# A delta-rule stage with copies, updates and weight pieces in another order on ScalarE and VectorE

## What is computed

```python
def even_mixer(h, w_in, conv_a_w, dn_conv_w, a_log, dt_bias, dn_norm_w, w_out):
    p = h @ w_in
    a_gate_in, a_gate_out, a_h, qkv, z, beta_raw, alpha_raw = jnp.split(p, splits, -1)
    y_a = a_gate_out * causal_dwconv(a_gate_in * a_h, conv_a_w)
    qkv = jax.nn.silu(causal_dwconv(qkv, dn_conv_w))
    ...
    beta = jax.nn.sigmoid(beta_raw.astype(jnp.float32))
    g = -jnp.exp(a_log) * jax.nn.softplus(alpha_raw + dt_bias)
    o = gated_delta_rule(padw(q), padw(k), padw(v), padw(beta), padw(g))[:, pad:]
    ...
def gated_delta_rule(q, k, v, beta, g):
    ...
    t_mat = a_strict + jnp.eye(c, dtype=jnp.float32)
    sol = lax.linalg.triangular_solve(t_mat, rhs, left_side=True, lower=True, unit_diagonal=True)
    def step(s, inp):
        v_new = u_n - jnp.einsum('bhcd,bhde->bhce', w_n, s)
        o = jnp.einsum('bhcd,bhde->bhce', qd_n, s) + jnp.einsum('bhij,bhje->bhie', qk_n, v_new)
        s = s * gl_n[..., None, None] + jnp.einsum('bhcd,bhce->bhde', kd_n, v_new)
```

## Time and profile before

| | us |
|---|---|
| median of 3 runs | 1295.26 |
| lowest and highest | 1292.99, 1295.29 |
| the profiled execution | 1298.23 |
| its span, first to last instruction | 1296.4 |
| busy: PE, DVE, ACT, POOL | 1257.5, 883.4, 666.7, 183.6 |
| mean granted clock of PE | 0.981 |

### The profile page before, as it was taken

How to read it: one execution, slowest core, us unless ns; L and a number is a source line. 1 busy time by engine, 2 the same in 40 slices (tenths; PEclk the granted TensorE clock), 3 DMA queues, 4 the chain that set the end, 5 groups by cost and what they waited for, 6 DMA issues and landing times.

```text
span 1296.4 us, 27179 instructions
## 1 busy us (share of the span) xinstructions
PE 1257.5 (97%) x10252; PEld 1223.7 (94%) x10252; DVE 883.4 (68%) x1640; ACT 666.7 (51%) x1189; POOL 183.6 (14%) x207
## 2 busy tenths in 40 slices
PE   6999999999999989999999999999999989999996
PEld 6989999999999879999999999999999968999996
DVE  7655468777745786888855776867555797866443
ACT  6635245555534564655534655655443576665331
POOL 0333114000012235000011001300011104000110
PEclk9979899999999998999999999999999999999998
DMA  7322227775654325555653444656556523655551
GB/s 281 95 70 78 70 82 221 212 203 178 213 173 133 100 75 165 192 182 183 216 192 124 150 144 131 211 181 188 182 180 194 197 82 90 204 181 178 192 186 59
DMA packets 60660, 206.38 MB, mean 159 GB/s; under 512 B 6176, under 2 KB 14624, under 8 KB 60448
## 3 DMA queue, kind: packets, MB, share of 16 engines
q1 hardware_dynamic: 56256, 200.85, 48.9%
q10 hardware_dynamic: 4320, 4.35, 1.1%
HBM read 200.99 MB, written 4.19 MB: 158 GB/s over the span
## 4 chain that ended last, share of the span: by engine, by line
PE 92%; DVE 5%; ACT 1%; issue 1%; DMA 1%; POOL 0%; POOLq 0%; DVEq 0%; SPq 0%; ACTq 0%
PE bank L311 27%; PE bank L313 27%; PE bank L312 27%; PE bank L1517 1%; PE bank L1540 1%; PE bank L1260 1%; PE bank L1530 1%; DVE w_lo L267 1%; PE bank L1258 1%; DMA raw<-w_mix_in 1%; PE bank L1245 1%; DVE sm_d L1558 1%; DVE sm_d L1580 0%; ACT w_hi L258 0%; DVE rstd L373 0%
## 5 line engine op out<-in xcount | busy, mean ns | idle before, releaser
L267 DVE TENSOR_TENSOR w_lo<-raw,w_hi 128x1024 fp32r<-128x1024 f32 (+1 forms) x358 | 459.0, 1283 | 200.7 <-ACT w_hi L258 199.5
L258 ACT ACTIVATE w_hi<-raw 128x1024 fp32r<-128x1024 f32 (+1 forms) x358 | 387.7, 1085 | 310.5 <-PE bank L313 288.0
L311 PE MATMUL bank<-x_hi,w_hi 128*128 128x256 f32 (+2 forms) x1784 | 517.6, 290 | 9.8 <-DVE x_lo L387 8.2
L313 PE MATMUL bank<-x_hi,w_lo 128*128 128x256 f32 (+2 forms) x1784 | 511.3, 287 | 0.0
L312 PE MATMUL bank<-x_lo,w_hi 128*128 128x256 f32 (+2 forms) x1784 | 511.2, 287 | 0.0
L311 PEld LDWEIGHTS bank<-x_hi,w_hi 128*128 128x128 f32 x1784 | 341.2, 191 | 12.2 <-DVE w_lo L267 8.1
L313 PEld LDWEIGHTS bank<-x_hi,w_lo 128*128 128x128 f32 x1784 | 341.3, 191 | 0.0
L312 PEld LDWEIGHTS bank<-x_lo,w_hi 128*128 128x128 f32 x1784 | 340.4, 191 | 0.4
L311 PE MATMUL bank<-m_hi,w_hi 128*128 128x256 f32 x512 | 144.1, 281 | 0.0
L312 PE MATMUL bank<-m_lo,w_hi 128*128 128x256 f32 x512 | 144.1, 281 | 0.0
L313 PE MATMUL bank<-m_hi,w_lo 128*128 128x256 f32 x512 | 144.1, 281 | 0.0
(11 more groups left out here) (302 smaller groups left out, 1736.1 us busy)
## 6 DMA issues: line engine op xcount, KB each, us to landing
raw<-w_up SPq DMA_DIRECT2D x88, 512.0 KB, 4.3
raw<-w_mlp_up SPq DMA_DIRECT2D x64, 512.0 KB, 4.2
raw<-w_mlp_down SPq DMA_DIRECT2D x64, 512.0 KB, 4.0
raw<-w_down SPq DMA_DIRECT2D x32, 704.0 KB, 4.1
raw<-w_mix_in SPq DMA_DIRECT2D x29, 512.0 KB, 3.6
raw<-w_moba_in SPq DMA_DIRECT2D x24, 512.0 KB, 4.0
raw<-w_swa_in SPq DMA_DIRECT2D x12, 512.0 KB, 3.5
raw<-w_mix_out SPq DMA_DIRECT2D x8, 512.0 KB, 3.6
```

The lines of the kernel that those rows point to most:

```text
L258: nc.scalar.activation(w_hi[:, slot, 0:WIDTHS[g]], raw[:, slot, 0:WIDTHS[g]], ACT.Copy).then_inc(hi_ready, 1)
L267: nc.vector.tensor_tensor(w_lo[:, slot, 0:WIDTHS[g]], raw[:, slot, 0:WIDTHS[g]], w_hi[:, slot, 0:WIDTHS[g]].bitcast(F32), ALU.subtract).th ...
L311: nc.tensor.matmul(out, whi, xh, start=(chunk == 0), stop=False)
L313: mm = nc.tensor.matmul(out, wlo, xh, start=False, stop=end)
```

## The change

The same instructions are issued with the same operands, except that ScalarE loads its activation table twice more. PE's and POOL's programs and SyncE's loads stay in their order. What moves:

- Norm: `round_(3)` goes behind `act_std` on ScalarE, `rest(3)` behind the first two evictions on VectorE; three pieces stand ahead of the norm in place of four.
- ScalarE, level 2: the `kd` rows of chunk 0 go up ahead of `silu(5)`, `p_copy(2)` ahead of `silu(6)`. From there `round_` stands ahead of the `tap3` of the next tile in place of behind it, and some silus go further back: `silu(7)` behind the four silus of `zs`, `silu(9)` behind the logarithm, `silu(11)` behind three groups of `q_exps`.
- ScalarE, level 6: the two `rows(bv, ...)` go behind `y_high(0)` and `glu_tap(1)`.
- VectorE, levels 2 to 4: `x_next` goes ahead of `conv(7)`, `conv(9)` and `conv(11)`, and each `rest` stays directly behind its eviction.

```diff
--- before.py
+++ after.py
@@ -789,11 +789,12 @@
                 if n == 2:
                     ins.then_inc(y_lo_ready, 4)
 
-            for t in range(4):
+            for t in range(3):
                 rest(t)
             dve_rstd(dve, name)
             evict_conv(0)
             evict_z(0)
+            rest(3)
             conv(0, between=1)
             rest(4)
             evict_z(1)
@@ -837,17 +838,27 @@
             nc.vector.tensor_scalar(negc[:], cexp[:, :, 4:8], -1.0, None, ALU.mult).then_inc(S("negc_ready"), 1)
             conv_slot(5)
             conv_slot(6)
-            conv_slot(7)
+            evict_conv(7)
+            rest(Q0 + 3)
             for n in chunks_at(2):
                 x_next(2, n)
-            conv_slot(8)
-            conv_slot(9)
+            conv(7)
+            evict_conv(8)
+            rest(V0)
+            conv(8)
+            evict_conv(9)
+            rest(V0 + 1)
             for n in chunks_at(3):
                 x_next(3, n)
-            conv_slot(10)
-            conv_slot(11)
+            conv(9)
+            evict_conv(10)
+            rest(V0 + 2)
+            conv(10)
+            evict_conv(11)
+            rest(V0 + 3)
             for n in chunks_at(4):
                 x_next(4, n)
+            conv(11)
             gate_in(0)
             rest(GLU0)
             gate_val(0)
@@ -988,9 +999,10 @@
                 nc.scalar.activation(o_std[0:c, 4 * n:4 * n + 4], SUMS[0:c, 4 * n:4 * n + 4], ACT.Sqrt,
                                      bias=eps[0:c, 0:1], scale=1.0 / P).then_inc(S("on_std"), 1)
 
-            for t in range(4):
+            for t in range(3):
                 round_(t)
             act_std(act, name)
+            round_(3)
             tap3(0)
             round_(4)
             tap3(1)
@@ -1038,41 +1050,41 @@
             for n in CHUNKS:
                 x_rows(n)
             rows(kd, K_ROWS, 2, 2, 8)
+            rows(kd, K_ROWS, 0, 3, 8)
             silu(5)
             tap3(6)
             round_(Q0 + 2)
-            rows(kd, K_ROWS, 0, 3, 8)
-            silu(6)
             for n in chunks_at(2):
                 p_copy(2, n)
+            silu(6)
+            round_(Q0 + 3)
             tap3(7)
-            round_(Q0 + 3)
-            silu(7)
             for k in range(4):
                 act.wait_ge(evac_done, lin.tile0 + Z_TILES[k] + 1)
                 nc.scalar.activation(zs[:, k, :], zs[:, k, :], ACT.Silu).then_inc(S("z_ready"), 1)
+            silu(7)
+            round_(V0)
             tap3(8)
-            round_(V0)
             for n in chunks_at(3):
                 p_copy(3, n)
             silu(8)
+            round_(V0 + 1)
             tap3(9)
-            round_(V0 + 1)
-            silu(9)
             act.wait_ge(S("l2_sum"), 2)
             nc.scalar.activation(ba[96:100, :], bank[7][96:100, 0:T], ACT.Ln, bias=eps[96:100, 1:2],
                                  scale=float(P)).then_inc(S("ls_ready"), 1)
+            silu(9)
+            round_(V0 + 2)
             tap3(10)
-            round_(V0 + 2)
             for n in chunks_at(4):
                 p_copy(4, n)
             silu(10)
+            round_(V0 + 3)
             tap3(11)
-            round_(V0 + 3)
-            silu(11)
             for hd in range(3):
                 q_exps(hd)
             round_(GLU0)
+            silu(11)
             for n in chunks_at(5):
                 p_copy(5, n)
             q_exps(3)
@@ -1083,11 +1095,11 @@
             round_(GLU0 + 3)
             for n in chunks_at(6):
                 p_copy(6, n)
-            rows(bv, V_ROWS, 1, 5, 0)
             y_high(act, "mix_out", 0, av[:, 0, :], 1)
             round_(GLU0 + 4)
+            glu_tap(1)
+            rows(bv, V_ROWS, 1, 5, 0)
             rows(bv, V_ROWS, 2, 6, 0)
-            glu_tap(1)
             round_(GLU0 + 5)
             for n in chunks_at(7):
                 p_copy(7, n)
```

## The result

| | before | after |
|---|---|---|
| median, us | 1294.12 | 1283.01 |
| lowest and highest | 1289.24, 1295.29 | 1281.42, 1283.68 |
| the profiled execution | 1298.23 | 1283.68 |
| its span | 1296.4 | 1281.8 |

The medians of four executions each lie 11.1 us apart, and the median after is 0.4 us from the predicted 1283.4. The measured ratio of the times is 0.9924, with an interval of 0.9907 to 0.9942; that is 9.8 us of 1294, somewhere between 7.5 and 12.0. The two profiled executions lie 14.55 us apart, more than the medians do. That difference between 14.5 and 10 to 11 turns out to be the instructive part of the case.

The account below looks back on a forecast made before the run. PE, busy 97% of the span, was taken as the bound, with time winnable only in its waits and half clock. 2.0 + 8.7 + 1.1 = 11.8 us off the median 1295.26 gave 1283.4 us, range 1279 to 1290.5.

Parts of the forecast that it names:

- Part B: Level 2: inverse copies straight behind the weight copy end PE's 2.72 us wait and the half clock behind it; 8.7 us.
- First copy by 67.1 at most: Level 2, ScalarE: the first inverse copy ends by 67.1, while PE is busy with its weight tile until 67.9.
- Hidden: Level 2, VectorE: with the update first, the next eviction can start at 75.3; PE needs its bank at some 84.
- VectorE becomes the bound: Rival, chance 0.06: late evictions or `w_lo` make PE wait, 8.7 us per place; two places give 1300.8 us.
- the clock falls at level 2 all the same: Rival, chance 0.15: products of 64 columns suffice for half clock, so only level 2's wait is won; 1289.4 us.
- The 5.9 us of clock: Level 2: full clock behind the ended wait wins 3.44 us in second(2) and 2.5 in the tile behind.
- Part C: Between levels 6 and 7: values' rows behind `y_hi` end PE's wait for `xt` ahead of first(7); 1.1 us.
- The clock of 144.92 to 151.75 I leave at half: Behind first(7): this half-clock stretch stays, since first(7) and the 16-row chunk's new values stay ahead of it; nothing won.
- the late stretches go too: Rival, chance 0.24: half clock from 144.92 goes, 3.1 us, perhaps the fourth stretch, 1.6 more; 1280.3, at best 1278.7 us.
- Part A: Norm: three weight pieces ahead shorten PE's wait for the first eviction and end half clock behind it; 2.0 us.
- The wait for `ba`: Gates, near 44: PE arrives earlier than VectorE's chain can follow, so a new wait of 0.6 us stays.
- The 1.56 us of clock: Behind the norm's wait: the 3.42 us half-clock stretch would take 1.86 at full clock, 1.56 won.

Follow-up runs that it names:

- b_act: Kernel before with only ScalarE's order of levels 2 to 4 changed (`pb` copies ahead of the silu, taps behind the weight copies): 1285.03 us, ratio 0.9946.
- c_only: Kernel before with only the values' rows moved behind `y_high` and the gate's tap on ScalarE: 1291.08 us, ratio 0.9982.
- a_only: Kernel before with only the norm's edit, the fourth weight piece moved behind the square root on ScalarE and two evictions on VectorE: 1294.72 us, ratio 1.0011.
- pcopy_back: Changed kernel with only the `pb` copies of level 2 put back behind `silu(6)` on ScalarE: 1291.37 us, ratio 0.9993.
- no_c: Changed kernel with the values' rows back ahead of `y_high` and the gate's tap on ScalarE: 1288.27 us, ratio 0.9971.
- inter: Changed kernel with pieces of two gate weight tiles mixed among PE's small matmuls of level 7: 1283.52 us, ratio 0.9940.
- after_again: Changed kernel, nothing altered, run again on the chip of the last three kernels: 1283.64 us, ratio 0.9934 to the kernel before.
- b_dve: Kernel before with only VectorE's order changed (updates of levels 2 to 4 ahead of a convolution, `rest` behind the eviction): 1292.33 us, ratio 1.0003.
- one_line: Kernel before with a single ScalarE edit, the `pb` copies of level 2 moved ahead of `silu(6)`: 1286.52 us, ratio 0.9960.
- no_a: Changed kernel with four weight pieces ahead of the norm again: 1284.62 us, ratio 0.9944.
- third group: Runs of after_again, gates, both and no_c on one chip, with 17 executions of the kernel before, whose median was 1290.39 us.
- gates: Changed kernel with one convolution tile's matmuls cut into three pieces around the gates' matmuls on PE: 1283.62 us, ratio 0.9936.
- both: Changed kernel with the PE edits of inter and gates together: 1282.63 us, ratio 0.9933.

## Why the prediction was right, and where it was not

The number was right, 1283.4 against 1283.01. The gain was forecast at 11.8 us and is 11.1 by the medians and 9.8 by the ratio. Point by point:

**Part B, 8.7 us: the mechanism right, the size that of the profile.** The traces differ by 8.71 us over its stretch; b_act alone won 7.0 and taking back its one line costs 7.6 to 8.9 us (0.9993 less 0.9934 or 0.9924, of 1292). First copy by 67.1 at most: it is at 64.16. second(2) takes 3.97 us, from 66.21 to its last pair at 70.18. "Hidden" for VectorE holds: its eviction is at 74.04, where I had 75.3. The rival "VectorE becomes the bound" is out; no wait for a convolution's eviction or a `w_lo` over 1 us is in the list. The other, "the clock falls at level 2 all the same", is out too: 1.00 from 25 to 140. The 5.9 us of clock belong to one execution, though: behind the same wait of 2.7 to 2.9 us stand 13.65 us at half clock in the profiles of before and c_only, 10.24 in those of a_only and pcopy_back, and 6.83 in that of b_dve.

**Part C, 1.1 us: the step that failed.** "The clock of 144.92 to 151.75 I leave at half", since small products stay in front of it. The traces won 1.21 for the wait and 2.97 for the clock behind it, and no_c, over twelve executions, shows it beside the changed kernel: 4.6 us (c_only, beside the kernel before, shows 2.3 and no less half clock). I had given this a chance of 0.24 as "the late stretches go too". It came about by half: one of the two late stretches, the one with the wait in front, went; the other, in which and before which PE was busy throughout, is still there at 140.45. My argument from that one to the other was wrong: that small matmuls can be followed by a fall without a wait did not mean that the wait did nothing.

**Part A, 2.0 us: the waits as reckoned, the clock term not shown.** Counted from PE's first matmul (8.16 and 8.54), the table load starts 1.23 us earlier (1.08 expected), and the first eviction ends after 15.51 us in place of 16.74. PE was ready for it in before at 24.96 - 1.63 = 23.33, that is after 15.17, so 0.4 us of the wait would be left, about the 0.5 forecast. That the trace of after has no wait at all is luck: the slow start brought PE there 0.9 us later. The wait for `ba` came as named, 0.37 for 0.6. From behind the start to the gates the traces differ by 1.26 + 1.52 = 2.8 us. But by its ratio part A alone is -1.4 us (1.0011, not told from nothing), and on top of B and C some 1.3 to 2.6, not told from nothing either. What I had not priced is that the place where the new wait stands has small matmuls behind it, and that the clock falls there: near 47 in the profiles of a_only, pcopy_back, inter and no_c, not in those of after and after_again.

The 1.56 us of clock that I booked for part A have a rival that I left untested. In the 14 traces the half clock behind the norm is in the five whose slow start was short (12 to 17 matmuls before the clock rises: before, b_dve, c_only, one_line, no_a), and in none of the nine where it was longer (20 to 27). All eight kernels with part A are among the nine, and so is b_act, without part A and with a wait of 1.15 us for `gb`. In after the clock rises at 14.2 us where I had 12. No run separates the wait from the slow start, or tells why that is longer in the kernels with part A.

**The clock terms and the base: two errors that met.** I had 1.56 + 5.9 = 7.5 us of clock, read from the profiled execution of before, with a granted clock of 0.981. Over its executions that clock goes from 0.981 to 0.992, and the time from 1298 to 1289. By the formula above the profiled one has 49 us at half clock, the mean one 34, and the 15 us between are 7.5 us of time. So for the mean execution the clock terms together were too large, and part C's missing 3 us made up for a part of it; the rest lies in the base, since 1295.26, the median of three, is 2.6 to 4.9 us above the medians of the larger groups. By the ratios the change is worth 8.5 us (third group) to 9.8 us, where I had 11.8. That the time came out within 0.4 us is in part luck. The sum against the profile itself (1286.4 for the 1283.68 measured) erred the other way.

The Trainium skill, "TensorE: Matmul & The Clock Gate", Part 1, calls the number of slow matmuls at the start variable from run to run. Here it goes from 12 to 27 over the traces, but those are of different kernels, and the two traces of the changed kernel have 25 and 24. By the page's account activity releases the throttle; the trace shows that the busy column alone doesn't tell when: PE is busy for all of 140.45 to 143.86, at 0.50.

**The parts don't add up.** Alone they give 7.0 (b_act), 0 (b_dve), 2.3 (c_only) and -1.4 (a_only) us, 7.9 together, near the 8.5 to 9.8 of the whole. Taken back one at a time they cost 7.6 to 8.9, 4.6 and 1.3 to 2.6 us, 13.5 to 16 together. And pcopy_back, with parts A and C in it, is only 0.9 us faster than the kernel before. The waits in the profiles come and go as I reckoned, so what doesn't add up should be the clock; which term of it, no run shows.

**What stays open.** A wait of 1.1 us ahead of first(7) was followed within some 5 us by half clock in the profiles of before, a_only, one_line and no_c, in that of b_dve only 8.5 us later, and in that of b_act not at all. Without the wait, after, after_again, no_a and pcopy_back have one late stretch of 3.41 us, and c_only, gates, inter and both none. With the wait there is more half clock beside the changed kernel (no_c against after_again); what decides it in one execution stays open, and so does the part of the slow start in it.

## What to carry to other kernels

A copy that PE waits for belongs straight behind what it reads, ahead of all work that itself waits for a third engine; one such line was worth 5 us here, and taking it alone back lost the gain of the whole reordering. A wait of 1 to 3 us on TensorE costs itself and often more again in the clock behind it (here 5.9 us behind 2.7, and 3.0 behind 1.1, in the traces), but price the clock from several executions: a single profile can be near the worst of them. A wait that is ended hands on to the next chain, so look at what stands behind that one before counting the gain.

## What the hardware showed that I had not expected

- The same program spreads over 10 us (1288.68 to 1298.39), with the granted clock from 0.992 to 0.981. Most of that is the clock: with half of the time at half clock taken off, the mean times of the second and the third group of before agree (1292.3 - 33.6 / 2 = 1275.5 and 1291.6 - 31.9 / 2 = 1275.6), and the change has 1283.3 - 22.6 / 2 = 1272.0. The 3.6 us between stand beside 5.0 us fewer of waiting in the profiles (5.4 less 0.4); the longer slow start, which this sum leaves out, gave back 0.9 of that in the trace of after.
- The clock falls after TensorE has been busy without a gap: from 134.00 to 140.40 PE is busy for all 6.40 us at 1.00, and then comes 140.45 to 143.86 at 0.50. Up to 137.1 that is a weight tile of matmuls with 272 columns, and behind it stand matmuls of 16 rows or of 64 and 128 columns (state_step, outputs, second(7) and the keys' product with the state). The kernel gates runs the same matmuls in the same order there, and its profile has no fall.
- A wait of 1.50 us (gates) was followed by a fall in one kernel's profile, and the same wait in the profile of both was not.
- The clock column reads 1.00 at the start of the span where the instruction counts show the slower pace (11 matmuls in 2.2 us in place of 19).
